# An mLSTM scan's steps on one core: gate rows broadcast as two f32r parts, query products on 64-row halves, the next step's products issued early

## The chip, the cores and the metric

One NeuronCore of one Trainium2 chip runs the whole kernel. The metric is the device time of one execution in microseconds. All data is float32 in memory; the large products are each made of three f32r products, of parts into which the operands are split.

## The reference, cut to what matters

Two layers act on 512 latent tokens and 256 context tokens of width 1024. Each layer has an input projection, four mixers side by side (two attentions, a gated linear attention called GLA, and an mLSTM), an output projection and an MLP. The change touches only the mLSTM: 4 heads of 64, both directions of the sequence. For each head and direction it computes, over chunks:

```
log_inter = F + m                               # F = cumulated log forget gate, m = running maximum
m_t  = max(log_inter, max(logw))                # logw[t,s] = F[t] - F[s] + i[s] for s <= t
w    = exp(logw - m_t);  w_inter = exp(log_inter - m_t)
qk   = (q @ k^T) * w
num  = qk @ v + w_inter * (q @ C);  den = sum(qk) + w_inter * (q @ n)
h    = num / max(|den|, exp(-m_t))
C    = decay * C + (w_end * k)^T @ v;  n = decay * n + sum(w_end * k)
```

The context tokens are scanned first and hand their state to the latent tokens. In the last layer the context's own outputs are not needed, its states are.

## The kernel before, in words

The kernel is written out engine by engine: each of TensorE, VectorE, ScalarE, GpSimd and the DMA queue on SyncE has its own program in a fixed order, and they meet at semaphores. In each layer the programs run `norm`, `in_proj` (the input projection, with the GLA and the gate preparation woven in as numbered small steps), `attention`, a joint stop (`stage_end`), `mlstm`, another stop, `finish`, the output projection and the MLP. Nothing of `mlstm` can therefore start before `attention` ends on all three engines, and `finish` cannot start before `mlstm` ends on all three.

The mLSTM works on tiles of 128 tokens: six steps s of `ORDER`, in each one tile j per direction d. A tensor `y_d` takes the output; the direction that reaches a tile second adds to what is there ("seen", two operations in place of one, in steps 1, 4 and 5). In layer 1 the two context steps, s = 0 and 1, only carry the state.

Before the steps TensorE transposes the keys (L3031), ScalarE copies them to `ktd` (L1267) and copies the queries into `qdb` (L1272), where each head has its 64 rows and VectorE has put zeros in the other 64 (L2082). Then, in each step, for direction d:

- TensorE writes a mask into PSUM bank d (L3046, bf16) and adds, with four float32 products (L3048, two instructions each), the row of running maxima `ft[12]` of each head, broadcast over 128 partitions. ScalarE makes the decays `wb` of it (L1284).
- TensorE forms the products of keys and queries for the four heads (L3055), with the zero-padded `qdb`. VectorE multiplies them into `wb` (L2101).
- VectorE weights the values (`vw`, L2093), TensorE forms the state's inflow (L3067), into bank d, and VectorE updates the state `cst_d` (L2109).
- TensorE forms query times state (L3080, again with `qdb`, 128 rows) and weights times values (L3083). VectorE scales the first (t1, L2119), adds the second (t2, L2120), forms the divisor (L2122, L2124, L2125) and the output (L2132, or L2128 and L2129 where the tile was seen).

TensorE's program takes both directions' mask, row and key products first, then both inflows, then L3080 and L3083 of each direction. It begins a step's L3046 only after the last state update.

The gate rows come from `mlstm_gates`, called on VectorE in `in_proj`; its last part ends with the semaphore `r_raw`. After it VectorE updates the GLA's states (L1865), for which the transposes L2770 on TensorE wait. GpSimd works in `in_proj` and on `finish_c` (L866, L869, L873), which in layer 0 ends at 360.5 us, and is idle from there until `finish` (L880).

Of the kernel before, what the change touches and what calls it, by code (L numbers as in the profile page):

```python
# [12 lines left out]
F32 = mybir.dt.float32  # L13
# [7 lines left out]
P = 128  # L21
# [67 lines left out]
C_KEEP = C_HM + 8  # L89
# [44 lines left out]
def build(nc, x_in, ctx_in, w_big, w_mod, vecs, consts, gla_gate, rows, out):  # L134
# [27 lines left out]
    p_before = keep("p_before", [P], BF16)  # L162
    vcol = [keep("vcol0", [V_ALL]), keep("vcol1", [LV1])]
# [30 lines left out]
    row2 = cst[:, C_HM + 4:C_HM + 6]  # L194

# [98 lines left out]
    qdb = place("qdb", RS, [4, T])  # L294
# [130 lines left out]


# [91 lines left out]
    with blk:  # L518
# [285 lines left out]
        def _(gp):  # L804
# [69 lines left out]

            def low_ab(l):

                n = n_q(l)
                for k in range(4):
                    gp.wait_ge(sem("y_hi"), 8 * l + k + 1)
                    nc.gpsimd.tensor_tensor(yT_lo[:, k, 0:n], yT_ab[:, k, 0:n], yT_hi[:, k, 0:n].bitcast(F32),  # L880
                                            ALU.subtract).then_inc(sem("yab_lo"), 1)

            for l in range(DEPTH):
                if l == 1:
                    low(l * PROJ + 1, 0)
                    gp.wait_ge(sem("h_ready"), KD + 6)
                low(l * PROJ + 2, 1)
                in_proj(l)
                finish_c(l)
                low_ab(l)  # L890
                lows(l * PROJ + IN_SLOTS + 2, (l + 1) * PROJ)

        @blk.scalar
        def _(act):
# [369 lines left out]
            def mlstm(l):  # L1264
                for a, n in ((0, 4), (4, 2)):
                    act.wait_ge(sem("kd_done"), T_("kd").add())
                    nc.scalar.activation(ktd[:, a:a + n, :], pair(a // 4, 0, n * 256).rearrange(  # L1267
                        "p (j c) -> p j c", j=n), ACT.Copy).then_inc(sem("ktd_ready"), 1)
                for p_ in range(2):
                    for hf in range(2):  # L1270
                        rr = slice(64 * hf, 64 * hf + 64)
                        nc.scalar.activation(qdb[rr, 2 * p_ + hf, 0:n_q(l)], ft[8 + p_][rr, 0:n_q(l)],  # L1272
                                             ACT.Copy).then_inc(sem("qdb_ready"), 1)
                k = 0
                for s in range(TILES):
                    for d in range(2):
                        j = ORDER[d][s]
                        if l == DEPTH - 1 and j >= LAT_TILES:
                            continue
                        act.wait_ge(sem("mb_done"), T_("mb").add())  # L1280
                        if k >= 4:
                            act.wait_ge(sem("num_done"), T_("num").n + k - 3)
# [4 lines left out]
                        k += 1  # L1287
                T_("num").add(k)
# [184 lines left out]
            for l in range(DEPTH):            x_total = 0  # L1473
# [66 lines left out]
        def _(dve):  # L1540
# [40 lines left out]
            def make_masks():  # L1581
# [3 lines left out]
                v.tensor_copy(ident_b[:], ident)  # L1585
                v.tensor_scalar(m_left[:], cload[:, C_LEFT - C_KEEP:C_LEFT - C_KEEP + P], -BIG, None, ALU.mult)
# [136 lines left out]
            def in_proj(l):  # L1723
# [21 lines left out]
                v.memset(vd1[:, :, :, 64:65], 1.0)  # L1745
# [167 lines left out]
            def mlstm_gates(l, part):  # L1913
# [50 lines left out]
                if part == 3:  # L1964
# [5 lines left out]
                    v.tensor_tensor(dec[R, :], mp[R, :], mend[R, :], ALU.subtract).then_inc(sem("r_raw"), 1)  # L1970

# [106 lines left out]
            def mlstm(l):  # L2078

                for h in range(4):  # L2080
                    a = 64 - 64 * (h % 2)
                    v.memset(qdb[a:a + 64, h, 0:n_q(l)], 0.0)  # L2082
                v.memset(cst_d[:], 0.0).then_inc(sem("qdb_zero"), 1)
                dve.wait_ge(sem("qdb_zero"), l + 1)
                seen = set()
                for s in range(TILES):
                    cur_, nxt = s % 2, (s + 1) % 2
                    for d in range(2):
                        j = ORDER[d][s]
                        if s < TILES - 1:  # L2090
                            if s >= 1:
                                dve.wait_ge(sem("ud_done"), T_("udv").add())
                            v.tensor_tensor(vw[:, d], vd1[:, j], bc(col[:, j, 0, 2 + d, :], 65),  # L2093
                                            ALU.mult).then_inc(sem("vw_ready"), 1)
                    if s == TILES - 1:
                        T_("udv").add(2)
                    outs = [d for d in range(2) if not (l == DEPTH - 1 and ORDER[d][s] >= LAT_TILES)]
                    for d in outs:
                        dve.wait_ge(sem("w_ready"), T_("w").add())
                        dve.wait_ge(sem("qk_done"), T_("qkd").add())  # L2100
                        v.tensor_tensor(wb[s % 2][:, d], wb[s % 2][:, d],  # L2101
                                        bank(2 + d).rearrange("p (h t) -> p h t", h=4),
                                        ALU.mult).then_inc(sem("p_ready"), 1)
                    for d in range(2):
                        j = ORDER[d][s]
                        if s < TILES - 1:
                            dve.wait_ge(sem("ud_done"), T_("ud").add())
                            for p_ in range(2):
                                last = v.scalar_tensor_tensor(  # L2109
                                    cst_d[:, d, nxt, p_, :], cst_d[:, d, cur_, p_, :], dcb[:, 2 * d + p_, j:j + 1],  # L2110
                                    bank(d, p_ * 65, 65), ALU.mult, ALU.add)
                            last.then_inc(sem("state_ready"), 1)
                            dve.wait_ge(sem("state_ready"), T_("st").add())
                    for d in outs:
                        j = ORDER[d][s]
                        dve.wait_ge(sem("num_done"), T_("num").add())
                        inter = bank(6 + d, 0, 260).rearrange("p (h c) -> p h c", h=4)
                        intra = bank(4 + d, 0, 260).rearrange("p (h c) -> p h c", h=4)
                        step(v.tensor_tensor(t1[:, d], inter, bc(col[:, j, 1, d, :], 65), ALU.mult))  # L2119
                        step(v.tensor_tensor(t2[:, d], t1[:, d], intra, ALU.add))  # L2120

                        step(v.scalar_tensor_tensor(dd[:, d, :], t2[:, d, :, 64], -1.0, t2[:, d, :, 64],  # L2122
                                                    ALU.mult, ALU.max))
                        step(v.tensor_tensor(dd[:, d, :], dd[:, d, :], col[:, j, 1, 2 + d, :], ALU.max))  # L2124
                        step(v.reciprocal(rd[:, d, :], dd[:, d, :]))  # L2125
# [8 lines left out]
                        dve.wait_ge(sem("yd_ready"), T_("yd").add())  # L2134
# [504 lines left out]
        def _(pe):  # L2639
# [387 lines left out]
            def mlstm(l):  # L3027
                for a, n in ((0, 4), (4, 2)):
                    for j in range(a, a + n):
                        for p_ in range(2):  # L3030
                            ins = nc.tensor.transpose(pair(a // 4, (j - a) * 256 + p_ * P, P),  # L3031
                                                      ft[10 + p_][:, cols(j)], ident)
                    ins.then_inc(sem("kd_done"), 1)
                pe.wait_ge(sem("ktd_ready"), T_("ktd").add(2))
                pe.wait_ge(sem("qdb_ready"), T_("qdb").add(4))
                pe.wait_ge(sem("qdb_zero"), l + 1)
                st0 = T_("st").n
                for s in range(TILES):
                    cur_ = s % 2
                    outs = [d for d in range(2) if not (l == DEPTH - 1 and ORDER[d][s] >= LAT_TILES)]  # L3040
                    if s >= 1:
                        pe.wait_ge(sem("state_ready"), st0 + 2 * s)
                    for d in outs:
                        j = ORDER[d][s]
                        mk = (p_after, p_before)[d]
                        mm(bank(d), ident_b[:], mk[:].unsqueeze(1).to_broadcast([P, 4, P]), start=True, stop=False)  # L3046
                        for h in range(4):
                            ins = mm(bank(d, h * P, P), sel[:, 4 * d + h:4 * d + h + 1].to_broadcast([P, P]),  # L3048
                                     ft[12][:, cols(j)], start=False, stop=(h == 3))
                        ins.then_inc(sem("mb_done"), 1)  # L3050
                        if T_("pk").n >= 1:

                            pe.wait_ge(sem("p_ready"), T_("pr").n)
                        for p_ in range(2):
                            ins = mm(bank(2 + d, p_ * 256, 256), ft[10 + p_][:, cols(j)],  # L3055
                                     qdb[:, 2 * p_:2 * p_ + 2, cols(j)], start=True, stop=True)
                        ins.then_inc(sem("qk_done"), 1)
                    if s < TILES - 1:
                        for d in range(2):
                            j = ORDER[d][s]  # L3060
                            pe.wait_ge(sem("vw_ready"), T_("vw").add())
                            if d in outs:
                                pe.wait_ge(sem("w_ready"), T_("w").add())
                            for h in range(4):
                                hf = h % 2
                                a = d * 512 + (h // 2) * 65
                                ins = mm(ps[64 * hf:64 * hf + 64, a:a + 65], ktd[:, j, h * 64:h * 64 + 64],  # L3067
# [401 lines left out]
```

## Time and profile before

| what | value |
|---|---|
| time, median of 3 runs | 1898.05 us (1892.0 to 1901.79) |
| span of the profiled execution, its only own time | 1892.3 us |
| TensorE busy | 1745.9 us, 92% |
| VectorE busy | 1207.3 us, 64% |
| ScalarE, GpSimd busy | 812.8 us (43%), 258.7 us (14%) |
| mean granted TensorE clock | 0.968 |
| mLSTM stage, layer 0 | 429.4 to 491.9 us |
| mLSTM stage, layer 1 | 1422.1 to 1470.8 us |

Times within the profile are counted from the start of the span. The granted clock is 1.00 for TensorE's upper level (2.4 GHz) and 0.50 for the lower (1.2 GHz). Matmul durations include their latency, so that instructions that follow each other overlap in the table; the chain of waits counts each moment once, and there the time per instruction is the rate at which they are issued.

### The profile page before, as it was taken

What the parts mean: (1) busy time and instruction counts of PE and PEld (TensorE: products, weight loads), DVE (VectorE), ACT (ScalarE), POOL (GpSimd) and SP (SyncE); (2) the same over time, 40 slices, a digit from 0 to 9 for tenths busy, and PEclk for the clock granted to TensorE, in tenths of its full rate; (3) what the DMA queues carried; (4) which work ended last, traced back from release to release, by engine and by line L of the source; (5) the groups of instructions that cost most, each with busy time, mean ns of one, the idle gap of its engine ahead of it and who ended that gap; (6) DMA issues with size and microseconds to landing.
All of it is one profiled execution on the core that took longest, in us unless ns stands there. A gap on an engine that the chain in (4) does not pass through costs nothing.

```text
span 1892.3 us, 29110 instructions
## 1 busy us (share of the span) xinstructions
PE 1745.9 (92%) x11904; PEld 1544.7 (82%) x11904; DVE 1207.3 (64%) x1761; ACT 812.8 (43%) x1178; POOL 258.7 (14%) x184
## 2 busy tenths in 40 slices
PE   6999999888897999999999988999888879999998
PEld 4778897667786989999899968779677678989797
DVE  5373736676528797896987955664666485647472
ACT  5333315642316733535435453233652264445261
POOL 0233622100220000000000023452200300000000
PEclk8899999998999999999999989999998989999999
DMA  9441113000055627457276123121200227455351
GB/s 372 154 158 47 46 45 134 1 1 1 7 195 211 234 91 301 176 183 295 71 285 232 44 70 129 69 99 57 112 1 1 112 102 276 152 204 211 123 179 45
DMA packets 43518, 247.18 MB, mean 131 GB/s; under 512 B 5604, under 2 KB 7050, under 8 KB 24714
## 3 DMA queue, kind: packets, MB, share of 16 engines
q1 hardware_dynamic: 43402, 245.55, 35.2%
q8 instruction: 83, 1.36, 0.3%
q14 instruction: 33, 0.27, 0.0%
HBM read 218.79 MB, written 26.74 MB: 130 GB/s over the span
## 4 chain that ended last, share of the span: by engine, by line
PE 70%; DVE 13%; ACT 7%; issue 4%; POOL 3%; DMA 3%; DVEq 0%; SPq 0%; ACTq 0%
PE ps L3236 19%; PE ps L3199 10%; PE ps L2745 9%; PE ps L2922 8%; PE ps L3158 5%; POOL w_lo L810 2%; PE ps L3002 2%; PE ps L2672 2%; DVE xT L2437 1%; DMA raw<-w_modl 1%; DVE w_lo L2391 1%; PE ps L3048 1%; DMA raw<-w_big 1%; PE ps L3055 1%; PE ps L2850 1%
## 5 line engine op out<-in xcount | busy, mean ns | idle before, releaser
L3236 PE MATMUL ps<-op_hi,w_hi 128*128 128x384 f32 x896 | 307.3, 343 | 21.3 <-DVE xT L2437 9.2
L810 POOL TENSOR_TENSOR w_lo<-raw,w_hi 128x512 fp32r<-128x512 f32 x124 | 175.3, 1445 | 958.4 <-ACT w_hi L916 935.8
L3236 PE MATMUL ps<-op_lo,w_hi 128*128 128x384 f32 x896 | 304.6, 340 | 0.0
L3236 PE MATMUL ps<-op_hi,w_lo 128*128 128x384 f32 x896 | 304.2, 339 | 0.0
L3236 PEld LDWEIGHTS ps<-op_hi,w_hi 128*128 128x128 f32 x896 | 170.7, 191 | 29.0 <-issue 26.2
L1390 ACT ACTIVATE w_hi<-raw 128x1024 fp32r<-128x1024 f32 x96 | 101.4, 1058 | 199.9 <-PE ps L3236 140.2
L3236 PEld LDWEIGHTS ps<-op_hi,w_lo 128*128 128x128 f32 x896 | 171.0, 191 | 0.0
L3236 PEld LDWEIGHTS ps<-op_lo,w_hi 128*128 128x128 f32 x896 | 170.8, 191 | 0.0
L1326 ACT ACTIVATE w_hi<-raw 128x1024 fp32r<-128x1024 f32 x80 | 82.3, 1052 | 147.5 <-PE ps L3199 126.2
L2922 PE MATMUL ps<-w_hi,h_hi 128*128 128x256 f32 x448 | 133.6, 298 | 5.6 <-POOL w_lo L810 5.6
L3158 PE MATMUL ps<-op_hi,w_hi 128*128 128x256 f32 x448 | 127.7, 285 | 8.4 <-DVE hid L2287 4.0
L2391 DVE TENSOR_TENSOR w_lo<-raw,w_hi 128x1024 fp32r<-128x1024 f32 x96 | 116.0, 1219 | 20.2 <-ACT w_hi L1390 20.1
L3158 PE MATMUL ps<-op_lo,w_hi 128*128 128x256 f32 x448 | 127.4, 284 | 0.0
L3158 PE MATMUL ps<-op_hi,w_lo 128*128 128x256 f32 x448 | 127.2, 284 | 0.0
L2922 PE MATMUL ps<-w_lo,h_hi 128*128 128x256 f32 x448 | 127.2, 284 | 0.0
L2922 PE MATMUL ps<-w_hi,h_lo 128*128 128x256 f32 x448 | 127.0, 283 | 0.0
L3199 PE MATMUL ps<-hid_hi,w_hi 128*128 128x512 f32 x256 | 102.2, 399 | 4.0 <-DVE hid_lo L2292 4.0
L2213 DVE TENSOR_TENSOR w_lo<-raw,w_hi 128x1024 fp32r<-128x1024 f32 x80 | 95.2, 1221 | 15.9 <-ACT w_hi L1326 15.9
L3199 PE MATMUL ps<-hid_hi,w_lo 128*128 128x512 f32 x256 | 101.5, 396 | 0.0
L3199 PE MATMUL ps<-hid_lo,w_hi 128*128 128x512 f32 x256 | 101.5, 396 | 0.0
L3158 PEld LDWEIGHTS ps<-op_hi,w_hi 128*128 128x128 f32 x448 | 86.2, 193 | 10.0 <-issue 9.9
L2922 PEld LDWEIGHTS ps<-w_hi,h_hi 128*128 128x128 f32 x448 | 85.3, 190 | 9.0 <-POOL w_lo L810 5.9
(370 smaller groups left out, 3977.4 us busy)
## 6 DMA issues: line engine op xcount, KB each, us to landing
raw<-w_big SPq DMA_DIRECT2D x96, 1024.0 KB, 6.1
raw_m<-w_modl SPq DMA_DIRECT2D x21, 1024.0 KB, 6.0
op_hi<-op_cache SPq DMA_DIRECT2D x21, 768.0 KB, 4.6
op_lo<-op_cache SPq DMA_DIRECT2D x21, 768.0 KB, 6.2
raw<-w_modl SPq DMA_DIRECT2D x14, 1024.0 KB, 5.0
op_hi<-op_cache SPq DMA_DIRECT2D x21, 512.0 KB, 4.0
op_lo<-op_cache SPq DMA_DIRECT2D x21, 512.0 KB, 5.4
first_mod<-w_modl SPq DMA_DIRECT2D x8, 1024.0 KB, 21.4
```

The source lines that it names most:

```text
L810: ins = nc.gpsimd.tensor_tensor(w_lo[r][:, ks, :], raw[0][:, ks, :], w_hi[r][:, ks, :].bitcast(F32), ALU.subtract)
L1326: nc.scalar.activation(w_part1(w_hi[r], P_, c_), w_part1(raw_of1(P_), P_, c_), ACT.Copy).then_inc(sem("mw_hi"), 1)
L1390: nc.scalar.activation(chunk(w_hi[r], c_), src, ACT.Copy).then_inc(sem("mw_hi"), 1)
L2213: v.tensor_tensor(w_part1(w_lo[r], P_, c_), w_part1(raw_of1(P_), P_, c_), w_part1(w_hi[r], P_, c_).bitcast(F32), ALU.subtract).then_inc(se ...
L2391: v.tensor_tensor(chunk(w_lo[r], c_), src, chunk(w_hi[r], c_).bitcast(F32), ALU.subtract).then_inc(sem("mw_lo"), 1)
L2672: ins = mm(ps[32 * g:32 * g + 32, at:at + WC], csw[:, k, :], w[:, k, :], start=(k < 4), stop=(k >= KD - 4))
L2745: ins = mm(pair(g, a, b - a), w[:, k, m * P:(m + 1) * P], mov[hl][:, k, a:b], start=(k == 0 and q == 0), stop=(k == KD - 1 and q == 2))
L2922: ins = mm(pair(g, (j - j0) * 256, 256), (h_hi, h_lo)[hl][:, k, cols(j)], w[:, k, :], start=(k == 0 and q == 0), stop=(k == KD - 1 and q = ...
L3002: ins = mm(ps[64 * hb:64 * hb + 64, 7 * 512 + p * P:7 * 512 + p * P + P], v_ab[:, kt, m * P + 64 * hb:m * P + 64 * hb + 64], probT[u % 2][ ...
L3158: ins = mm(bank(base + g, 0, HALF1), wide(w)[:, k, g * P:(g + 1) * P], ops[hl][:, k, :], start=(P_ in FRESH and k == 0 and x == 0), stop=( ...
L3199: ins = mm(bank(4 + g % 4), w[:, k, m * P:(m + 1) * P], (hid_hi1, hid_lo1)[hl][:, k, :], start=(k == 0 and x == 0), stop=(k == KD - 1 and ...
L3236: ins = mm(bank(base + g, 0, h), wide(w)[:, k, g * P:(g + 1) * P], ops[hl][:, k, 0:h], start=(p in FRESH and k == 0 and q == 0), stop=(k = ...
```

## The change

It does the following.

- The row of maxima is split on VectorE, in `mlstm_gates`, into a part rounded to f32r and a remainder, stacked in `row_parts`, and GpSimd (`spread_rows`, between `finish_c` and `low_ab`) multiplies each tile's rows by a mask that leaves one head per 128 columns. One f32r product of 512 columns then broadcasts all four heads of a direction.
- `qdb`, its zeros and its copies are gone. The key-query and the query-state products take the 64 rows of each head from `ft[8..11]`; the even heads write one PSUM bank, the odd heads another (banks 2, 3 and 6, 7).
- The state's inflow moves to columns 260 to 389 of banks 4 and 5. TensorE's order becomes: inflow of s, query-state of s, mask and rows of s+1, weights-values of s, key-query of s+1. ScalarE makes the decays of s+1 early.
- VectorE's order becomes: weighting of both directions, state updates, `vw` of s+1, t1 and t2, the divisors of both directions at once, the outputs. t1 takes two operations per direction, since its input lies in two banks.

The core of the diff:

```diff
@@ mlstm_gates, VectorE, after r_raw
+                    dve.wait_ge(sem("r_raw"), l + 1)
+                    step(v.tensor_copy(row_parts[64:128, :], gates[0:64, :]))
+                    v.tensor_tensor(row_parts[0:64, :], gates[0:64, :], row_parts[64:128, :].bitcast(F32),
+                                    ALU.subtract).then_inc(sem("rows_split"), 1)
+                    dve.wait_ge(sem("rows_split"), l + 1)
@@ GpSimd
+            def spread_rows(l):
+                gp.wait_ge(sem("rows_split"), l + 1)
+                gp.wait_ge(sem("big_done"), slot_done(l * PROJ + IN_SLOTS - 1))
+                for j in range(n_q(l) // P):
+                    if j == 3:
+                        gp.wait_ge(sem("msc_ready"), l + 1)
+                    ins = nc.gpsimd.tensor_tensor(spread[j // 3][:, j % 3], row_parts[:, cols(j)].bitcast(F32).unsqueeze(1)
+                                                  .to_broadcast([P, 4, P]), bc(row4, P), ALU.mult)
+                ins.then_inc(sem("spread_ready"), 1)
@@ VectorE, mlstm(l)
+                    if reads(l, s):
+                        for d in range(2):
+                            dve.wait_ge(sem("w_ready"), out_n(l, s, d))
+                            dve.wait_ge(sem("qk_done"), out_n(l, s, 1))
+                            w = wb[s % 2][:, d].rearrange("p (b f) t -> p b f t", f=2)
+                            v.tensor_tensor(w, w, qk_of(d), ALU.mult).then_inc(sem("p_ready"), 1)
+                    if s < TILES - 1:
...
+                        if s < TILES - 2:
+                            weigh_values(s + 1)
...
+                        dve.wait_ge(sem("num_done"), out_n(l, s, d))
...
+                            dve.wait_ge(sem("inter_done"), inter_n(l, s, 1))
+                            for hf in range(2):
+                                last = v.tensor_tensor(
+                                    t1[:, d, hf::2, :], bank(6 + hf, 2 * d * 65, 130).rearrange("p (b c) -> p b c", b=2),
+                                    bc(col[:, j, 1, d, hf::2], 65), ALU.mult)
+                            last.then_inc(sem("inter_ready"), 1)
+                            dve.wait_ge(sem("inter_ready"), inter_n(l, s, d))
+                            v.tensor_tensor(t2[:, d], t1[:, d], intra, ALU.add).then_inc(sem("sum_ready"), 1)
@@ TensorE, rows_out, query_key and the order of mlstm(l)
+                        mm(bank(d), ident_b[:], mk[:].unsqueeze(1).to_broadcast([P, 4, P]), start=True, stop=False)
+                        mm(bank(d), of_group[:, d:d + 1].to_broadcast([P, P]), spread[j // 3][:, j % 3],
+                           start=False, stop=True).then_inc(sem("mb_done"), 1)
...
+                        for p_ in range(2):
+                            for hf in range(2):
+                                r = slice(64 * hf, 64 * hf + 64)
+                                ins = mm(bank(2 + hf, (2 * d + p_) * P, P), ft[10 + p_][r, cols(j)],
+                                         ft[8 + p_][r, cols(j)], start=True, stop=True)
...
+                for s in range(TILES):
+                    if s < TILES - 1:
+                        inflow(s)
+                    if s > 0 and reads(l, s):
+                        inter(s)
+                    if s + 1 < TILES and reads(l, s + 1):
+                        rows_out(s + 1)
+                    if reads(l, s):
+                        intra(s)
+                    if s + 1 < TILES and reads(l, s + 1):
+                        query_key(s + 1)
```

In the new order `inflow(s)` waits, per direction, for `vw` of s, the state of s-1 and t2 of s-1; `intra(s)`, which writes the banks of the inflow, waits for the weighting and for the state of s.

## Rows read from the trace of the kernel before

**Rows 1.** The page: the chain of waits by engine.
```profile
PE 70%; DVE 13%; ACT 7%; issue 4%; POOL 3%; DMA 3%; DVEq 0%; SPq 0%; ACTq 0%
```
**Rows 2.** Chain of waits, one step of layer 0: start us, us, what.
```profile
446.76 0.22 PE ps L3046
446.97 0.89 PE ps L3048 x8
447.86 0.87 PE ps L3055 x4
...
450.70 0.38 PE ps L3067 x8
...
451.61 1.04 PE ps L3080 x8
452.65 0.89 PE ps L3083 x8
...
455.33 0.21 PE ps L3046
```
**Rows 3.** Timeline of VectorE in the steps: start us, us, engine, line, [idle before].
```profile
449.06 0.77 DVE L2093 TENSOR_TENSOR vw<-vd,col 128x260 f32<-128x260 f32 x2
...
451.65 0.98 DVE L2109 SCALAR_TENSOR_TENSOR cst_d<-cst_d,dcb,ps 128x65 f32<-128x65 f32 x4
...
453.65 0.43 DVE L2119 TENSOR_TENSOR t<-ps,col 128x260 f32<-128x260 f32 x1 [1.02 <-PE ps L3083]
454.11 0.42 DVE L2120 TENSOR_TENSOR t<-t,ps 128x260 f32<-128x260 f32 x1
...
454.57 0.17 DVE L2122 SCALAR_TENSOR_TENSOR dd<-t 128x4 f32<-128x4 f32 x1
...
455.18 0.42 DVE L2128 TENSOR_TENSOR hh<-t,rd 128x256 f32<-128x256 f32 x1
...
459.23 1.28 DVE L2101 TENSOR_TENSOR wb<-wb,ps 128x512 f32<-128x512 f32 x2
```
**Rows 4.** Chain of waits: the last operation of the mLSTM stage in each layer.
```profile
491.47 0.43 DVE y_d L2129
...
1470.35 0.43 DVE y_d L2129
```
**Rows 5.** Timeline of all engines at the stage's start in layer 0.
```profile
429.45 2.59 PE L3031 MATMUL ps<-cst,ft 128*128 128x128 f32 x12 [1.04 <-DVEq L1557]
...
432.68 3.43 ACT L1272 ACTIVATE qdb<-ft 64x768 f32<-64x768 f32 x4
...
436.21 0.59 PE L3046 MATMUL ps<-p_after,ident_b 128*128 128x512 bf16 x1 [4.17 <-ACT qdb L1272]
...
438.54 1.14 ACT L1284 ACTIVATE wb<-ps,col 128x128 f32<-128x128 f32 x4 [2.43 <-PE ps L3048]
```
**Rows 6.** Timeline of TensorE in attention (64-row products), then chain of waits, output projection (f32r).
```profile
1407.18 0.48 PE L2955 MATMUL ps<-ft,ft 64*128 64x256 f32 x1
1407.18 0.48 PE L2960 MATMUL ps<-ft,ft 64*128 64x256 f32 x1
...
1488.63 11.48 PE ps L2745 x48
```
**Rows 7.** Timelines in layer 1's `in_proj` (VectorE, TensorE) and layer 0's attention (VectorE).
```profile
1200.55 0.95 DVE L1969 SCALAR_TENSOR_TENSOR r<-ft 36x768 f32<-36x768 f32 x1
...
1205.39 0.85 PE L2770 MATMUL ps<-cst,r 128*128 128x128 f32 x6 [0.94 <-DVE snap L1865]
...
357.74 1.81 DVE L2018 TENSOR_REDUCE nb<-ps 128x1 f32<-128x768 f32 x2
```
**Rows 8.** Busy time by stretch (PE, PEld, DVE, ACT, POOL), granted clock, DMA share, GB/s.
```profile
376.00:378.00 2.00, 0.88 (x7) 0.50 (x5) 1.83 (x7) 1.51 (x4) 0.00 (x0) 1.00 0.00 0
378.00:380.00 2.00, 1.89 (x9) 1.09 (x9) 0.00 (x0) 0.05 (x1) 0.00 (x0) 0.63 0.04 8
...
442.00:450.00 8.00, 7.93 (x73) 7.42 (x73) 6.06 (x20) 1.71 (x7) 0.00 (x0) 1.00 0.01 2
```

More of the change, by code:

```diff
@@ L1266, in mlstm, with decays @@
                     act.wait_ge(sem("kd_done"), T_("kd").add())
-                    nc.scalar.activation(ktd[:, a:a + n, :], pair(a // 4, 0, n * 256).rearrange(
+                    nc.scalar.activation(ktd[:, a:a + n, :], bank(4 + a // 2, 0, n * 256).rearrange(
                         "p (j c) -> p j c", j=n), ACT.Copy).then_inc(sem("ktd_ready"), 1)
[L1269 to L1275, printed above, removed]
+                def decays(s):
                     for d in range(2):
                         j = ORDER[d][s]
[L1278 to L1282, printed above, removed]
+                        act.wait_ge(sem("mb_done"), out_n(l, s, d))
+                        if s >= 2 and reads(l, s - 2):
+                            act.wait_ge(sem("num_done"), out_n(l, s - 2, d))
                         for h in range(4):
@@ L2088, in mlstm @@
+                    if not reads(l, s):
+                        continue
                     for d in range(2):
                         j = ORDER[d][s]
[L2090 to L2096, printed above, removed]
@@ L2114, in mlstm @@
[L2114 to L2125, printed above, removed]
@@ L3036, in mlstm, with rows_out @@
[L3036 to L3043, printed above, removed]
+                def rows_out(s):
+                    for d in range(2):
                         j = ORDER[d][s]
@@ new lines, in inflow @@
+                def inflow(s):
+                    for d in range(2):
+                        j = ORDER[d][s]
+                        pe.wait_ge(sem("vw_ready"), step_n(l, s, d))
+                        if s >= 1:
+                            pe.wait_ge(sem("state_ready"), step_n(l, s - 1, d))
+                        if s >= 1 and reads(l, s - 1):
+                            pe.wait_ge(sem("sum_ready"), out_n(l, s - 1, d))
+                        for h in range(4):
+                            hf = h % 2
+                            a = (4 + d) * 512 + 260 + (h // 2) * 65
+                            ins = mm(ps[64 * hf:64 * hf + 64, a:a + 65], ktd[:, j, h * 64:h * 64 + 64],
+                                     vw[:, d, h, :], start=True, stop=True)
+                        ins.then_inc(sem("ud_done"), 1)
@@ new lines, in inter @@
+                def inter(s):
+                    for d in range(2):
+                        j = ORDER[d][s]
+                        pe.wait_ge(sem("state_ready"), step_n(l, s - 1, d))
+                        if s > 1 and reads(l, s - 1):
+                            pe.wait_ge(sem("inter_ready"), inter_n(l, s - 1, 1))
+                        for p_ in range(2):
+                            for hf in range(2):
+                                r = slice(64 * hf, 64 * hf + 64)
+                                ins = mm(bank(6 + hf, (2 * d + p_) * 65, 65), ft[8 + p_][r, cols(j)],
+                                         cst_d[r, d, s % 2, p_, :], start=True, stop=True)
+                        ins.then_inc(sem("inter_done"), 1)
@@ L3082, in mlstm, with intra @@
+                def intra(s):
+                    for d in range(2):
+                        j = ORDER[d][s]
+                        pe.wait_ge(sem("p_ready"), out_n(l, s, d))
+                        if s < TILES - 1:
+                            pe.wait_ge(sem("state_ready"), step_n(l, s, d))
                         for h in range(4):
@@ L3416, in _constants @@
             c[32 * h:32 * h + 32, C_HM + h] = 1.0
-    for i in range(2):
+    for i in range(4):
         c[:, C_HM + 4 + i] = p % 32 == i
+    for d in range(2):
+        c[:, C_GROUP + d] = p // 32 % 2 == d
     s_, t_ = p[:, None], p[None, :]
```

133 lines of the change are left out of this document (71 added, 62 removed).

## The prediction

> **What bounds the kernel now.** I read the chain of waits first: TensorE holds 70% of it, VectorE 13% [rows 1]. Within the mLSTM stage the chain, read in order of time, shows TensorE line after line without a gap. One step of layer 0 runs from one L3046 to the next but one, 446.76 to 455.33, that is 8.57 us [rows 2]. The reader should see in these rows that every group is at TensorE's own rate, so that the step is as long as TensorE's list. For one direction the list is 0.22 (mask), 0.89 (rows), 0.87 (key-query), about 0.42 (inflow), 0.89 to 1.04 (query-state), 0.89 (weights-values), some 4.3 us; two directions give the 8.57. Next I read VectorE's timeline in the same steps: it waits only about 1.0 us per step for L3083 [rows 3], so it is the next engine to bind, and close behind.
>
> The last row of each stage ends at 491.9 and 1470.8 us [rows 4]. Both stages are walls for all engines: what a step or the start gives back moves everything after it, because `finish`, the weight splits and the DMAs of the output projection are released by events behind the wall.
>
> **TensorE's list after the change.** The four float32 row products (0.89) become one f32r product of 512 columns; the output projection issues such products at 11.48/48 = 0.24 us [rows 6]. The key-query products become eight instructions of 128 columns on two row halves. In attention two 64-row products on different halves start at the same 1407.18 and last the same 0.48 [rows 6], so I take halves as running in pairs: L3055 spends 0.87 for four of 256 columns; eight of 128 in pairs take half of it, 0.43. Query-state likewise: eight instructions took 0.89, in pairs 0.45. Sum for two directions: 2 x (0.22 + 0.24 + 0.43 + 0.42 + 0.45 + 0.89) = 5.3 us. The bound from the other side is that halves don't pair: 2 x (0.43 + 0.44) more, 7.0 us. I take 5.3, the nearer row.
>
> The row for switching shapes is the 1.04 of L3080 behind the 64-column L3067, against 0.89 of L3083 behind L3080 [rows 2]: some 0.15 at a switch. The Trainium skill, TensorEngine Tiling (Array Packing), section Key Properties, says that changing the tiling mode drains the engine, which speaks against this change, as it now changes shape four or five times a step. The trace agrees in sign; with 0.15 each the list is 6.0 us instead of 5.3, still below VectorE's, so the sum does not move.
>
> **VectorE's list after the change**, start to start, from [rows 3]. The two weightings: 1.28 for both, 1.20 to the next start. State updates 0.98. `vw` 0.77, 0.69 to the next start. t1 was one operation of 260 elements, 0.43 and 0.46 to its dependent (453.65 to 454.11); two of 130 are not in the trace. Between L2109 (four of 65 in 0.98, 0.25 each) and 0.43 I take 0.25 for the first and 0.37 for the second: 0.62 a direction; bounds are 0.46 (nothing added) and 0.86 (two full ones). t2 0.38 where nothing waits, 0.46 at the end. So 2.08 for both directions. Divisor: three small operations at 0.20, now once, 0.60 (before twice). Output 0.80 for both directions where unseen, 1.72 where seen (four of 0.42, 455.18 and its like, at 0.46, less one overlap). Sum: 1.20 + 0.98 + 0.69 + 2.08 + 0.60 = 5.55, plus 0.80 = 6.35, or plus 1.72 = 7.27. These exceed TensorE's 5.3 to 6.0: VectorE becomes the bound.
>
> Added waits. `intra(s)` waits for the state of s; behind it in TensorE's queue stand key-query of s+1 and the next inflow. From the end of direction 0's state, TensorE needs 0.1 to start and VectorE can read 1.22 after that (L3083's eight and their latency); VectorE meanwhile does the other state and `vw`, 0.48 + 0.69 = 1.17. The stall is some 0.1 a step. `inflow(s)` waits for t2 of s-1, and has the divisor, the outputs and the weighting, over 2.6 us, to finish its 0.8. ScalarE's 1.14 per direction is a step ahead. So steps of 6.45 and 7.4 (7.3 to 7.4; I use 7.3).
>
> **Layer 0.** Before the steps ScalarE's copies of the queries cost 3.43 us and TensorE stood idle for 4.17, falling to 0.5 clock, where L3046 took 0.59 [rows 5]. Now TensorE goes from the transposes (end about 431.9) straight to rows and key-query of step 0, at the low clock: 1.75 + 1.7, until 435.4. ScalarE copies `ktd` to 432.8, then decays 2 x 1.14 [rows 5], 435.3. Weighting to 436.8, the two first states 437.3, `vw` 438.0; weights-values of both directions are there at 439.3, t2 ends at 439.7. Then 6.45, 7.3 (step 1's outputs are seen), 6.45, 6.45: 466.35. The last step has no state: outputs of step 4, 2.32; first weighting 0.69; start 0.1; 1.22; t1 and t2 1.00, and 1.08 for the other direction: 6.41. Then divisor and outputs 2.32: 475.1. The end was 491.9: 16.8 us are gained.
>
> **Layer 1.** The stage starts at 1422.1. The order of its start is as in layer 0, in two context steps without outputs. The query copies gone, the first inflow starts at 1425.0. Two inflows (0.9), the rest of the states' 0.98 and `vw` 0.69 bring step 1's inflow to 1426.8 and its end to 1428.0; rows of step 2 at the low clock (1.75) to 1429.8, key-query (1.7) to 1431.5; the decays (2 x 1.14) end at 1431.4. Then, as in layer 0, inflow 1.6 (low clock), query-state and rows of step 3 (2.4, the clock rising), weights-values and VectorE's t2 of both directions (3.2): 1438.7. Then 2 x 6.45, 6.41 and 2.32: 1460.3, against 1470.8, a gain of 10.5 us.
>
> **What it costs elsewhere.** The split of the rows is two VectorE operations on 64 x 768. The nearest row has 36 x 768 at 0.95 [rows 7]; with the waits 1.7 us, bounds 0.8 (a copy at double rate) and 2.0. In layer 0 VectorE then waits for TensorE for more than that, and the cost is hidden; without that cover it is 1.7. In layer 1 TensorE's L2770 already waits 0.94 us for the GLA states behind it [rows 7], so it waits 1.7 longer. I charge 1.7 once. GpSimd's `spread_rows` is six and four operations of 512 elements in attention, where GpSimd is idle; its own end is needed 55 us later. VectorE reads mostly PSUM there: L2018 takes 0.91 each beside a running GpSimd operation [rows 7], as it does alone. I take nothing; the bound is all of it in VectorE's way, ten operations at about 1.5, 15 us. No DMA is moved.
>
> **Sum.** 16.8 + 10.5 - 1.7 = 25.6. The profile's own span is 1892.3, so 1866.7; it lies 5.75 below the median of the runs shown, and the same gain from 1898.05 gives 1872.4. I predict 1872 us. About 0.5% (9.5 us) is what a measurement here can tell from no change.
>
> **Rivals.**
> A, the clock falls inside the steps. With VectorE as the bound TensorE idles some 1 to 2 us in each step. For: in attention TensorE was busy 0.88 of 2 us and the next stretch shows 0.63 [rows 8]. The Trainium skill, TensorE: Matmul & The Clock Gate, section on the second HAM failure mode, says the same, that frequent small idles between groups make the clock oscillate; the trace shows it there once. Against: the full clock lasted through most of attention, with gaps of 1 us in 3. A fall that lasts 4 us (I take the stretch of the start of layer 0, 436 to 440) costs 2 us of TensorE's time; five of them cost 10 us: 1882.
> B, halves don't pair. TensorE's list is 7.0 + 0.7 for switches = 7.7, and binds in the unseen steps, and inflow, query-state and rows (0.9 + 1.9 + 0.9) come 0.4 to 0.6 late for weights-values: about 1 us in each of 10 steps, 1882 to 1883. Against it stand [rows 6].
> C, GpSimd is in VectorE's way in attention, up to 15 us: 1887. Against it [rows 7].
> D, slower than before: the clock stays at 0.5 through all steps. TensorE's list then is 2 x 5.3 + 0.6 = 11.2 against 8.57. Layer 0: 441.5 + 5 x 11.2 + 2.3 = 499.8, layer 1: 1440 + 3 x 11.2 + 2.3 = 1475.9; with 1.7 that is 7.9 + 5.1 + 1.7 = 14.7 slower, 1913. It decides from about two thirds of the steps' time at the low level. Against: TensorE would then never idle, and when it was that busy the level came back (1.00 throughout 442 to 450) [rows 8].
>
> **From these the numbers.** Forecast 0.70 (its own range 1862 to 1880), A 0.14, B 0.07, C 0.04, D 0.05. Runs spread by some 5 us about their median. The range 1862 to 1887 leaves out D, part of C and a run below the forecast's own range. Faster by over 0.5% (below 1888.6): the forecast and nearly all of A and B, 0.88; same: C and the rest of A and B, 0.07; slower: D, 0.05.
>
> **What would show it.** Key-query and query-state at half the time of before in the chain; the f32r row product near 0.24. In the steps the chain should pass to VectorE and TensorE should show idle released by VectorE. Steps near 6.4 and 7.3. The stages 45.7 and 38.2 us long. Granted clock 1.00 from about 435 on. L2770 in layer 1 waiting 2.6. The prediction is wrong if a step is still above 7.5 with TensorE in the chain, if the clock column shows 0.5 inside the steps, or if attention grows.

## The result, and the profile after

The changed kernel takes 1867.07 us (median of 4 runs, 1863.81 to 1873.26) beside 1897.27 for the kernel before on the same chip: ratio 0.984, 95% interval 0.982 to 0.987. The forecast was 1872 (1862 to 1887), faster. The profiled execution took 1863.81 us, its span is 1862.0; the span before was 1892.3, so 30.3 us went. Compared stage by stage, the mLSTM stage of layer 0 gave 19.0, that of layer 1 gave 13.5; the start and layer 0's attention, which the change hardly touches, differ by 2.2 more, between the stages 3.9 came back, and behind them 0.5: -19.0 - 13.5 - 2.2 + 3.9 + 0.5 = -30.3.

The chain of waits by engine, over the whole kernel: TensorE has gone from 70% to 68, VectorE from 13% to 15 [rows 1].
```profile
PE 68%; DVE 15%; ACT 7%; issue 5%; POOL 3%; DMA 3%; SPq 0%; DVEq 0%; ACTq 0%
```
One step of layer 0 in the chain (start us, us, what), against the gapless TensorE list of [rows 2]:
```profile
455.51 0.44 DVE t L2169
...
456.38 0.21 DVE rd L2176
...
456.96 0.43 DVE y_d L2185
...
458.02 0.68 DVE wb L2137
458.70 0.40 DVE cst_d L2147 x2
459.10 0.14 issue
459.23 1.98 PE ps L3145 x16
461.21 0.02 issue
461.24 0.51 DVE t L2164 x2
461.74 0.02 issue
461.77 0.44 DVE t L2169
```
From one L2169 to the next the step is 6.26 us, and the chain goes in a circle: divisor, outputs, weighting and direction 0's state on VectorE, 0.14 until TensorE starts, the weights-values products, then t1 and t2. `vw` is not in it. VectorE's timeline of the same step answers to [rows 3]: between the states and t1 it waits 0.88 us. This step, the last but one, has no `vw`; in the others the 0.77 us of `vw` lie in that wait. In layer 1 two periods at full clock, one with `vw` and one without, take 6.25 and 6.26 us (t2 starts at 1418.52, 1424.77 and 1431.03).
```profile
456.62 0.76 DVE L2185 TENSOR_TENSOR y_d<-t,rd 128x256 f32<-128x256 f32 x2
457.42 1.28 DVE L2137 TENSOR_TENSOR wb<-wb,ps 128x512 f32<-128x512 f32 x2
458.62 0.85 DVE L2147 SCALAR_TENSOR_TENSOR cst_d<-cst_d,dcb,ps 128x65 f32<-128x65 f32 x4
460.35 0.49 DVE L2164 TENSOR_TENSOR t<-ps,col 128x130 f32<-128x130 f32 x2 [0.88 <-PE ps L3145]
```
TensorE's timeline gives its list start to start: weights-values 1.82, key-query 1.09, inflow 0.62, query-state 1.04, masks and rows 0.92 (452.14 to 453.06), in sum 5.49 us.
```profile
452.14 0.39 PE L3094 MATMUL ps<-p_after,ident_b 128*128 128x512 bf16 x1
452.17 0.58 PE L3095 MATMUL ps<-spread,of_group 128*128 128x512 f32 x1
...
453.06 1.89 PE L3145 MATMUL ps<-vd,wb 128*128 128x65 f32 x16
454.88 1.16 PE L3106 MATMUL ps<-ft,ft 64*128 64x128 f32 x16
455.97 0.69 PE L3121 MATMUL ps<-vw,ktd 128*64 128x65 f32 x16
456.59 1.11 PE L3134 MATMUL ps<-cst_d,ft 64*128 64x65 f32 x16
457.63 0.39 PE L3094 MATMUL ps<-p_after,ident_b 128*128 128x512 bf16 x1
```
The granted clock, by stretch (columns as in [rows 8]), fell once between the products of layer 0's steps, right behind the idle of step 1, which is 1.43 us long (444.52 to 445.95):
```profile
444.00:446.00 2.00, 0.57 (x4) 0.18 (x2) 1.97 (x7) 1.91 (x8) 0.00 (x0) 1.00 0.02 4
446.00:448.00 2.00, 2.00 (x16) 2.00 (x16) 1.77 (x6) 0.27 (x2) 0.00 (x0) 0.85 0.04 8
448.00:450.00 2.00, 2.00 (x18) 1.88 (x17) 1.53 (x8) 0.00 (x0) 0.00 (x0) 0.50 0.00 0
450.00:452.00 2.00, 2.00 (x36) 1.71 (x32) 1.97 (x5) 0.00 (x0) 0.00 (x0) 0.79 0.00 0
```
The row split, and the wait that it lengthens in layer 1 to 3.92 us (0.94 before [rows 7]):
```profile
1181.54 0.55 DVE L2009 CAST row_parts<-ft 64x768 fp32r<-64x768 f32 x1
1182.13 0.95 DVE L2010 TENSOR_TENSOR row_parts<-ft,row_parts 64x768 fp32r<-64x768 f32 x1
```
```profile
1186.93 0.85 PE L2823 MATMUL ps<-cst,r 128*128 128x128 f32 x6 [3.92 <-DVE snap L1902]
```

### The profile page after: what moved, and what is told of

Same layout as the page of the kernel before. It is cut to its first block, busy times and chain, and to the rows that moved or that the text cites. A ratio compares the mean times of both kernels' runs of the same rounds, so it can differ in the third digit from the quotient of the medians.

```text
span 1862.0 us, 28947 instructions
## 1 busy us (share of the span) xinstructions
PE 1712.9 (92%) x11828; PEld 1509.6 (81%) x11828; DVE 1197.5 (64%) x1738; ACT 807.1 (43%) x1170; POOL 268.5 (14%) x194
## 4 chain that ended last, share of the span: by engine, by line
PE 68%; DVE 15%; ACT 7%; issue 5%; POOL 3%; DMA 3%; SPq 0%; DVEq 0%; ACTq 0%
PE ps L3314 20%; PE ps L3277 10%; PE ps L2798 9%; PE ps L2975 8%; PE ps L3236 5%; POOL w_lo L838 2%; PE ps L2725 2%; PE ps L3055 2%; DVE xT L2490 1%; DVE w_lo L2444 1%; DMA raw<-w_modl 1%; DVE mx L2063 1%; PE ps L3145 1%; DMA raw<-w_big 1%; PE ps L2903 1%
## 5 line engine op out<-in xcount | busy, mean ns | idle before, releaser
L838 POOL TENSOR_TENSOR w_lo<-raw,w_hi 128x512 fp32r<-128x512 f32 x124 | 174.9, 1441 | 961.0 <-ACT w_hi L956 938.5
```

The costliest lines, as they stand in the source:

```text
L838: ins = nc.gpsimd.tensor_tensor(w_lo[r][:, ks, :], raw[0][:, ks, :], w_hi[r][:, ks, :].bitcast(F32), ALU.subtract)
```

## The experiments

Theory after the first measurement: a step is VectorE's circle of 6.25 us (7.17 where outputs are seen), TensorE's list has 0.75 us of room in it, and the gaps on TensorE cost clock. Rivals: VectorE's busy sum sets the period; TensorE's list does; being a step ahead makes the gain.

The table has every run. Stage lengths are from the start of the first weighted values to the end of the last t2 of the profiled execution, the period is the one between t2s at full clock. In the changed kernel's first profile the stages are 41.1 and 32.7 us. Times are to be compared by the ratio: the kernel before had medians of 1896.56, 1895.89 and 1897.67 us beside the three groups of four.

| kernel | median us (range) | ratio to before, 95% | layer 0, layer 1 us | period us |
|---|---|---|---|---|
| a_again | 1866.82 (1861.1 to 1874.2) | 0.9852, 0.9827 to 0.9878 | 41.1, 34.3 | 6.25 |
| b_f32_rows | 1866.35 (1862.9 to 1867.6) | 0.9846, 0.9828 to 0.9864 | 44.2, 34.8 | 6.80 |
| c_no_ahead | 1864.19 (1861.1 to 1870.0) | 0.9840, 0.9819 to 0.9860 | 45.1, 30.6 | 6.26 |
| d_vw_gpsimd | 1873.85 (1865.3 to 1876.8) | 0.9873, 0.9851 to 0.9895 | - | 6.26, 7.04 |
| e_late_split | 1866.67 (1858.6 to 1873.5) | 0.9843, 0.9820 to 0.9865 | 50.3, 31.1 | 6.25 |
| f_y_gpsimd | 1854.50 (1851.9 to 1862.9) | 0.9793, 0.9773 to 0.9812 | 36.0, 30.2 | 5.50 |
| g_qk_twice | 1871.04 (1863.2 to 1873.6) | 0.9858, 0.9839 to 0.9877 | 44.2, 33.2 | 6.38 |
| h_late_y | 1853.67 (1850.2 to 1856.5) | 0.9781, 0.9767 to 0.9796 | 36.0, 28.7 | 5.50 |
| i_y_no_ahead | 1859.33 (1853.6 to 1866.0) | 0.9795, 0.9769 to 0.9821 | 39.6, 30.5 | 5.90 |
| j_y_f32 | 1866.32 (1861.3 to 1869.1) | 0.9828, 0.9808 to 0.9849 | 45.7, 33.9 | 6.80 |
| k_fill_step | 1859.11 (1858.3 to 1862.5) | 0.9801, 0.9783 to 0.9818 | 40.3, 33.7 | 6.25 |
| l_h_fill_end | 1851.71 (1848.4 to 1855.0) | 0.9757, 0.9738 to 0.9776 | 36.0, 30.3 | 5.50 |

**a_again**, the yardstick. 

> The changed kernel once more, nothing altered: the yardstick for the others of this chip. Both theories: about 1866 us beside 1897 (its trace before: span 1862.0), first mLSTM stage 43.5 us and second 35.1 us long, steps 6.25 us apart.

The same time as at first. Its executions differ with the mean clock: 1861.13 and 1863.82 us at 0.970, 1873.40 and 1874.21 at 0.960. In its profile layer 1's stage is 1.6 us longer than in the first, as the clock was at 0.50 in the last step (a period of 7.80 us for 6.12).

**b_f32_rows.**
```diff
-    mm(bank(d), of_group[:, d:d + 1].to_broadcast([P, P]), spread[j // 3][:, j % 3], ...)
+    for h in range(4):
+        ins = mm(bank(d, h * P, P), sel[:, 4 * d + h:4 * d + h + 1].to_broadcast([P, P]), ft[12][:, cols(j)], ...)
```


> The gate rows go back to four float32 products a direction, at the place where the changed kernel has its one f32r product; the split on VectorE and its ten spreading operations on GpSimd fall away, all else stays. Theory (a step is a loop through VectorE that leaves TensorE only some 0.35 us: list of 5.9 us in a period of 6.25): the eight float32 products were about 0.22 us each before, so the list becomes some 7.2 us and binds, +0.9 to +1.0 a step over nine steps, so +8 to +9 us in the stages, and -1.7 us at the input projection of layer 1, in sum +6 to +8 us. Rival 1 (TensorE has room, the rows cost nothing): 0 in the stages, -1.7 in sum. Rival 2: the rows lengthen the loop itself twice over: over +12 us.

The period grows by 0.55 us only. TensorE, now with next to no gap, gives its list: rows 2.22 instead of 0.92.
```profile
450.04 0.39 PE L3088 MATMUL ps<-p_after,ident_b 128*128 128x512 bf16 x1
450.27 1.05 PE L3090 MATMUL ps<-ft,cst 128*128 128x128 f32 x8
...
452.26 1.90 PE L3141 MATMUL ps<-vd,wb 128*128 128x65 f32 x16
```
So 5.49 + 1.30 = 6.79, the measured 6.80: the theory's mechanism holds, with my list 0.4 too long. In the whole the time is the same, not +6. Two things pull the other way in the profile: the split's cost goes, and the clock stayed at 1.00 through the steps of layer 0 (424 to 466); how much each gave isn't shown. The f32r row, for which rows are split and spread, bought nothing in this kernel.

**c_no_ahead.**
```diff
-    if s + 1 < TILES and reads(l, s + 1): rows_out(s + 1)  ...  query_key(s + 1)
+    if reads(l, s): rows_out(s); query_key(s)   # first in step s
```


> The rows and the key-query products of a step are issued at its own start instead of a step ahead; the instructions are the same. Theory (VectorE's loop, from outputs through weighting, state and weights-values products to the outputs, sets the period; the rows need only the weights of the step before): +0 to +0.3 us a step, at most +3 us. Rival (being a step ahead is what makes the gain): rows, exponentials (about 0.8 us each and their waits) and weighting then come one after the other in a step, about +2 us a step, so +15 to +20 us.

As the theory has it: periods of 6.26, 6.25 and 6.13 us in layer 1, time the same. Layer 0 is longer because its clock was at 0.50 at the start and fell twice more.

**d_vw_gpsimd.**
```diff
-    v.tensor_tensor(vw[:, d], vd1[:, j], bc(col[:, j, 0, 2 + d, :], 65), ALU.mult)
+    nc.gpsimd.tensor_tensor(vw[:, d], vd1[:, j], bc(col[:, j, 0, 2 + d, :], 65), ALU.mult)
```


> The weighting of the values (two operations a step) moves from VectorE to GpSimd, waits as before. Theory (on VectorE it lies in the shadow of the wait for the weights-values products, and the loop does not pass through it): steps within 0.1 us of 6.25, time within 1 us of the changed kernel's. Rival (VectorE's busy sum sets the period): -0.7 us a step, so about -6 us.

The undisturbed period of 6.26 is one that has no `vw` in the changed kernel either. What tells is the period of 7.04, which has one there: the outputs are 0.79 us longer, and with `vw` gone from VectorE the wait between the states and t1 is still 0.88. So `vw` is not in the circle and the busy sum doesn't bind. But I missed two costs. Beside GpSimd's operation the outputs take twice their 0.76 us (VectorE, then GpSimd, layer 1):
```profile
1429.58 1.55 DVE L2187 TENSOR_TENSOR y_d<-t,rd 128x256 f32<-128x256 f32 x2
1431.16 1.28 DVE L2141 TENSOR_TENSOR wb<-wb,ps 128x512 f32<-128x512 f32 x2
...
1434.10 0.49 DVE L2166 TENSOR_TENSOR t<-ps,col 128x130 f32<-128x130 f32 x2 [0.88 <-PE ps L3147]
```
```profile
1429.47 1.38 POOL L921 TENSOR_TENSOR vw<-vd,col 128x260 f32<-128x260 f32 x2 [4.29 <-PE ps L3123]
```
The Trainium skill, SBUF — State Buffer, section Who interferes with whom, says that a VectorE instruction with two SBUF inputs contends with a GpSimd instruction that reads SBUF. The trace agrees: the outputs read SBUF twice, and both engines lost, VectorE 0.79 us and GpSimd 0.18 (1.38 for 1.20). The second cost: in layer 0 TensorE stood idle for over 2 us (none busy from 446 to 448), and then the clock stayed at 0.50 from 450 to the stage's end, with periods of 10.13 us. By the medians the kernel is 7 us slower than a_again, but the intervals overlap.

**e_late_split.**
```diff
+                    if q == 20:   # behind the first gate_columns, in in_proj
+                        step(v.tensor_copy(row_parts[64:128, :], gates[0:64, :])) ...
```


> The split of the gate rows (two operations on VectorE) moves from before the input projection of layer 1 to a place behind the first gate columns, inside that projection. Theory: the wait of 3.92 us ahead of the first float32 projection matmuls of layer 1 goes back to between 0.9 and 2.2 us, -1.7 us in sum, nothing lost elsewhere. Rival: VectorE is late there anyway and the split only moves, within 0.3 us of the changed kernel.

The wait goes from 2.83 us (a_again; 3.92 at first, as TensorE came to it 1.1 us earlier) to 1.11, that is -1.72, and from these products to their second group it takes 7.15 instead of 8.70 us, -1.55 more. First e, then a_again:
```profile
1193.62 0.85 PE L2825 MATMUL ps<-cst,r 128*128 128x128 f32 x6 [1.11 <-DVE snap L1909]
...
1200.77 0.82 PE L2825 MATMUL ps<-cst,r 128*128 128x128 f32 x6
```
```profile
1186.67 0.85 PE L2823 MATMUL ps<-cst,r 128*128 128x128 f32 x6 [2.83 <-DVE snap L1902]
...
1195.37 0.82 PE L2823 MATMUL ps<-cst,r 128*128 128x128 f32 x6
```
The 1.55 are the clock's. Behind the longer wait it fell in a_again; in e it stayed at 1.00 there. a_again:
```profile
1180.00:1190.00 10.00, 7.17 (x55) 7.00 (x55) 8.21 (x18) 5.11 (x7) 4.54 (x4) 0.90 0.00 0
1190.00:1200.00 10.00, 10.00 (x92) 9.53 (x95) 4.10 (x8) 0.00 (x0) 1.67 (x2) 0.93 0.46 159
```
The shares missing from 1.00 make 1.7 us of these 20. Of the profiles with the early split, whose waits are 2.81 to 3.92 us, all but c have this second price (c takes 7.21 us between the groups at a clock of 1.00); of the five with the late split or none, where the wait is 1.11 or 1.12, none has.

Yet the time is the same within its interval. The profiled execution shows one thing that may hide it: the instructions of layer 0's stage are those of a_again, but after the same idle the clock did not come back, though TensorE was busy without a gap:
```profile
442.00:444.00 2.00, 0.57 (x5) 0.32 (x3) 2.00 (x7) 2.00 (x8) 0.00 (x0) 1.00 0.01 4
444.00:446.00 2.00, 2.00 (x16) 2.00 (x14) 1.55 (x5) 0.03 (x1) 0.00 (x0) 0.74 0.04 8
446.00:456.00 10.00, 10.00 (x70) 8.72 (x69) 5.88 (x19) 2.17 (x8) 0.00 (x0) 0.50 0.00 0
456.00:466.00 10.00, 10.00 (x69) 8.72 (x69) 5.19 (x17) 2.17 (x8) 0.00 (x0) 0.50 0.01 2
```
Periods of 10.13 us, and a stage 9.2 us longer than a_again's (50.3 - 41.1): rival D of the prediction, in one layer of one execution. The Trainium skill, TensorE: Matmul & The Clock Gate, section Seeing it yourself, tells of a gate seen stuck at a quarter of the clock. Here it was half, from 446 to 482 us, and the periods bear the column out.

**f_y_gpsimd.**
```diff
-    step(v.tensor_tensor(hh[:, d], t2[:, d, :, 0:64], bc(rd[:, d, :], 64), ALU.mult)) ...
+    nc.gpsimd.tensor_tensor(hh[:, d], t2[:, d, :, 0:64], bc(rd[:, d, :], 64), ALU.mult) ...   # all steps but the last
```


> The products with the reciprocal and their sums (two to four operations a step, 0.42 us each on VectorE) of all steps but the last go to GpSimd; VectorE waits for GpSimd once a step before it writes the next sums over their operands. Theory (they lie in VectorE's loop, which is all that sets 6.25 us): the period falls to TensorE's list, 5.9 to 6.0 us, where GpSimd's four operations at 1.0 to 1.2 us each fit into it; seven periods at -0.3 and the unread steps at -0.8, -3 to -5 us in the stages. Rival 1 (GpSimd has its operations done too late for the next sums, or slows VectorE beside it): periods of 6.5 to 7.5 us, +3 to +10 us. Rival 2: TensorE stands longer before the products and its clock falls through the first stage as where the weighted values went to GpSimd (periods near 10 us): +8 us and more.

More than expected: 0.9793 against 0.9852 and 0.9843, 12.3 us by the medians. Of the same 12.3 between the profiled spans 5.1 lie in layer 0's stage and 4.1 in layer 1's, where 1.7 are the clock of a_again's last step; the other 3.1 lie outside the stages and are not explained. The periods are 5.61, 5.40 and 5.50 us, on average TensorE's list to 0.01, and TensorE has no gap (12.00 busy of 12):
```profile
434.00:446.00 12.00, 12.00 (x160) 10.58 (x157) 10.78 (x36) 4.34 (x16) 3.97 (x6) 1.00 0.01 3
```
GpSimd's two outputs at 0.6 us each run beside the weighting, which has one input in PSUM and takes 1.25 us, as alone.

**g_qk_twice.**
```diff
-    for p_ in range(2):
+    for p_ in (0, 1, 0, 1):
```


> The key-query products of every step are issued twice over (the second pair writes the same result again), +1.1 us on TensorE a step, nothing on VectorE. The float32 rows added 1.3 us to the same list and the period went from 6.25 to 6.80 us, so theory (list 5.7 us in a period of 6.25, the rest exposed): +0.5 to +0.6 a step here too, periods of 6.7 to 6.9, +5 us in the stages. Rival (it was not TensorE's list but the rows' own delay ahead of the exponentials that made 6.80): 6.25 to 6.4 us, within 1 us.

+0.13 a step, not +0.5: the second set costs 0.89, 5.49 + 0.89 = 6.38 is the measured period, and 0.13 of it shows over VectorE's 6.25. My list was 0.2 to 0.4 too long, and the reading by which b had shown an exposed part was wrong; b, f and g together fix one list: 6.80 - 1.30 = 5.50 = 6.38 - 0.88.

**h_late_y**, e and f together. 

> The late split and the outputs on GpSimd together. Theory: the sum of both, -5 to -7 us beside the changed kernel. Rivals: as for each alone; if the outputs on GpSimd lose, this shows it once more at other clock dips.

0.9781 beside f's 0.9793: the outputs' gain is there again; what the late split adds is within the intervals.

**i_y_no_ahead**, c and f together. 

> The outputs on GpSimd, and the rows and key-query products at the start of their own step instead of a step ahead. Theory (being a step ahead cost nothing to give up only because VectorE's loop hid it; with TensorE's list of 5.50 us as the period, rows, exponentials and weighting lie ahead of the weights-values products in the loop): periods of 6.0 to 6.7 us instead of 5.50, +5 to +9 us beside the outputs on GpSimd alone, so about 1860 to 1863 us. Rival (the rows of a step need only the step before's weights, so TensorE still finds them in time): 5.5 to 5.6 us, within 2 us of 1854.5.

Between the two: 5.90 us. Now VectorE waits for the key-query products (0.46 us ahead of the weighting), and TensorE for the state. Being a step ahead is worth 0.4 us a step once the outputs are gone; the whole times don't tell the two apart.

**j_y_f32**, b and f together. 

> The outputs on GpSimd, and the gate rows by float32 products, without the split and the spreading. Theory (with the float32 rows TensorE's list is 6.80 us and was already the period with the outputs on VectorE): periods stay 6.80, nothing of the 0.75 us a step is gained; 1864 to 1866 us, some +10 beside the outputs on GpSimd with the f32r rows. Rival (the loop, not the list, made 6.80): 6.0 to 6.3, about 1858 us.

As the theory has it: 6.80 us, and 0.9828 is b's 0.9846 within the intervals. The f32r row is worth 1.30 us a step (6.80 to 5.50), but only behind the outputs' move.

**k_fill_step.**
```diff
-    for p_ in range(2):
+    for p_ in ((0, 1, 0, 1) if s in (2, 5) else (0, 1)):
```


> The changed kernel with one set of key-query products issued a second time in two places, ahead of the idle of steps 1 and 4 (0.9 us each on TensorE; the result is the same). Theory (TensorE's idle of 1.4 us in step 1 is what its clock falls after): the granted clock stays 1.00 through the first stage, step 2 takes 6.25 instead of 6.7 us and step 1 7.2 instead of 7.5, the stage ends about 1 us earlier; in executions where the level stayed at 0.50 for the rest of the stage (periods 10.13) up to 9 us are saved, so the median falls by 1 to 4 us beside 1866.7. Rival (the falls come at their own times, whatever TensorE does there): no change, or +1 us for the added work.

The clock stays at 1.00 until the stage's last products, the periods are 7.17, 6.26, 6.25 and 6.13 us. The stretch that had 0.57 busy now has
```profile
440.00:442.00 2.00, 1.46 (x10) 0.74 (x9) 2.00 (x7) 1.20 (x5) 0.00 (x0) 1.00 0.01 4
442.00:444.00 2.00, 2.00 (x21) 1.93 (x22) 1.77 (x8) 0.97 (x4) 0.00 (x0) 1.00 0.04 8
```
With work added the kernel was not slower, and probably faster: 0.9801 against a_again's 0.9852, intervals apart, but 0.9783 to 0.9818 just meets the 0.9816 to 0.9871 of the first measurement. By the medians it is 7.7 us, where 1 to 4 were expected, and the range is 4.2 us wide instead of 13.

That the filled idle made all of this is not shown. The two profiled spans differ by 8.0 us. Only 0.8 of them lie in layer 0's stage (40.3 against 41.1). 4.1 lie ahead of it, where the two programs are the same (it starts at 423.04 instead of 427.15), 2.5 between the stages and 0.6 behind. Executions like the one that e showed, each worth some 9 us, would fit the narrower range, but how often they happen I can't say, as one execution of a kernel is profiled. Against it, f has no gap in these steps and still ranges over 11 us, with mean clocks from 0.964 to 0.972.

**l_h_fill_end.**
```diff
+                for _ in range(3):   # behind the last weights-values products: key-query of the last step, both directions
```


> Late split and outputs on GpSimd, and behind the last weights-values products of each stage three more sets of key-query products (2.6 to 3.0 us), in the 4.45 us that TensorE waits for the end of the stage. Theory (the clock falls after that idle, and the output projection's first products run at 0.5 for some 6 us): the clock stays at 1.00 there, -2 to -3 us in each layer, about 1848 to 1850 us. Rival (the projection waits there for weights and features anyway): within 1 us of 1853.7, or later by what the added products overrun.

The clock stays at 1.00 (462 to 480), but from the last output to the end of the first projection's wait it is 11.67 us with and without the added products: 463.05 to 474.72 in h's chain, 467.68 to 479.35 here. That time is GpSimd's:
```profile
472.65 6.66 POOL yT_lo L961 x2
479.31 0.04 issue
479.35 6.62 PE ps L3254 x36
```
So the rival was right about the place. The 0.9757 is the best time of all, its interval touches h's.

## Why the prediction was right, and where its sizes were off

- **The bound passes to VectorE**: right, shown by c, d, f, g. The step is 6.25 us, not 6.45: t1 and t2 of both directions take 1.88 instead of 2.08. Seen steps are 7.17 (k) against 7.3. I had added VectorE's list, with a stall of 0.1; the circle leaves out `vw` and the other direction's state, 1.17 us in the prediction, and has 0.14 and TensorE's 1.12 in their place, for which the prediction had 0.1 and 1.22. The two sums are nearly the same here, but only the circle tells that moving `vw` gains nothing (d).
- **TensorE's list**: 5.49, between 5.3 and 6.0. Halves pair: key-query 0.55 a direction (0.43 forecast, 0.87 before), query-state 0.52 (0.45), inflow 0.31 (0.42). Rival B falls. In g the second set of key-query products took 0.88 where the first takes 1.09: the own rate is 0.44 a direction, the forecast's number, and some 0.2 is spent on coming to the group from another one, near the 0.15 that I took; that it is the shape, no run separates. The whole list stands only 0.2 over 5.3, as the inflow was forecast too long by as much.
- **Layer 0's start**: mis-sized. I took its clock at 0.5; the idle of [rows 5] was gone and it stayed at 1.00, so the first t2 ended 8.3 us after the stage's start instead of 10.3. That and the periods make 19.0 of the forecast 16.8, even with a fall of the clock in step 2. In the profiles of c, d, g, i and j the start was at 0.50 after all, as forecast.
- **Layer 1**: 13.5 instead of 10.5: 2.5 at the start, which took 14.1 us to t2 of step 2 instead of 16.6, and the rest in the steps.
- **The split**: 1.72 us by e, 1.7 forecast; in layer 0 it is hidden, as forecast (L2823 starts at 159.10, L2770 at 159.09 before). A term was left out: the longer wait can cost the clock, 1.55 us in the next stretch of the projection (all but c of the kernels with the early split). The wait was to be 2.6 and was 3.92 and 2.83.
- **`spread_rows`**: 1.0 us each, not 1.5, and attention is no longer than before. Rival C falls for this change; d shows that its mechanism exists.
- **Given back**: forecast was the split's 1.7, measured 3.9 between the stages. In the output projection of layer 0 the DMA landed 20.5 us earlier (517.73 for 538.18), but the clock was lower in the stretch behind it and the same 48 products took longer, so some 2.4 us went:
```profile
507.28 10.45 DMA raw<-w_modl
...
518.85 10.19 PE ps L2798 x48
```
The like of it before took 8.52 us. Up to the split's wait in layer 1 these were made good again (TensorE comes to it at 1183.01 for 1204.45, 21.4 us ahead), the wait took 3.0 of them, and from there to the stage 1.1 more went.
- **Rivals A and D**: the prediction called itself wrong if the clock column shows 0.5 inside the steps, and it does. A's fall came once in layer 0 of the profiled execution and cost about 0.8 us (7.53 + 6.66 against 7.17 + 6.25), too little to move the sum; D's low level came in e and d for a stage's rest. I gave them 0.14 and 0.05 as things that happen to a kernel; e beside a_again shows that they happen to an execution. The spread goes with the mean clock, but where in the kernel its falls lie is seen for one execution each: in the profiles whose program is the same up to there (the changed kernel, a, c, d, f, g, i, k) the first stage starts anywhere from 421.8 to 427.2 us. The 2.2 us that the start gave are less than that, and may be luck.

What made the gain was thus not all that was changed. Rows in f32r (b) and the step ahead (c) bring nothing until the outputs leave VectorE. What is left to carry it are the key-query and query-state products on halves (1.09 + 1.04 us a step for two directions against 1.74 + some 1.93), the copies gone and VectorE's new order. None of these three was undone by itself, so their shares rest on the traces before and after. An estimate from these rows: with the old products the list would be 5.49 + 1.54 = 7.03 us, above VectorE's 6.25.

## What to carry to other kernels

When several engines pass one step around, find the circle that the chain repeats, and price each operation by whether it lies on it: moving `vw` off VectorE gained nothing, moving the outputs gained 12 us. Two improvements of the same step can each be worth nothing until the other's bound is gone (b against j), so try them in pairs. TensorE, given idles of 1 to 4 us, may lose its clock behind them, and such an idle then costs more than its length (the split's 1.55). Filling one with work that nobody needs cost nothing here (k), and is worth a try.

## What the runs showed of the hardware that I had not expected

- Behind an idle of 1.43 us in a loop TensorE's granted clock fell to 0.50 (the 1.2 GHz level). In a_again it was back at 1.00 by 452, in e it stayed at 0.50 from 446 to 482, though TensorE was busy for 20.00 of the 20 us from 446 on. With the idle filled to some 0.5 us it stayed at 1.00 (k).
- The same stretch of program has the fall in one execution and not in another: behind a wait of 2.8 us in layer 1's projection the clock fell in a_again, d and k and not in c.
- Two VectorE multiplications on SBUF beside GpSimd ones took twice their time (1.55 for 0.76), a weighting with an operand in PSUM did not (1.25 for 1.28). In e the split fell beside GpSimd's weight parts (L838) and took 1.44 and 1.93 us for 0.55 and 0.95.
